# A hybrid attention encoder: half of the third branch's attention weights are transposed by VectorE and a DRAM round trip, the other half where they lie

## The chip, the cores and the metric

The kernel runs on one core of a Trainium2 chip. The metric is the device time of one launch in microseconds (us), the median of three runs. A core has five engines with an instruction queue each: TensorE (PE), VectorE (DVE), ScalarE (ACT), GpSimd (POOL) and SyncE (SP). SP does nothing here but issue DMAs. Engines meet only at semaphores, and each runs its own instructions strictly in order.

## The reference

Two layers over a sequence of 512 tokens with 1024 channels. Each layer normalizes x, projects it, runs three token mixers side by side, gates and merges them, and adds the result to x. The second and the third mixer turn attention weights:

```python
# B: differential attention, 4 heads of two maps each
s = einsum('bhtqd,bhtkd->bhtqk', qblk, k) * scale
p = softmax(s, axis=-1)
w = p[:, :, 0] - lam * p[:, :, 1]
o = einsum('bhqk,bhke->bhqe', w, v)
# C: dilated windows, 8 heads; three patterns (window, dilation),
# each a masked softmax, merged by a softmax over the three log-sums
s = where(valid, s, -1e30)
lse = logsumexp(s, axis=-1); p = exp(s - lse[..., None])
wts = softmax(stack(lses), axis=0)
o_c = einsum('gbhs,gbhsd->bhsd', wts, stack(outs))
```

The merge of C equals one softmax over all 512 keys whose scores carry the logarithm of how many patterns see the key; the kernel computes it so, with a mask of logarithms (`lmask`).

## The kernel before

Each layer has three stages: the norm of x, four *groups* of heads, then the branch and output projections. A group i holds one GLA head, one B head and two C heads, and 18 tiles of the input projection: four of values (`v0` to `v3`), `a`, `bq` to `ck`, the gates `ag`, `bg`, `cg` and the merge gates `m0` to `m5`. The first group of a layer is written out and the other three run in a loop, so a layer's groups hold the same work. A product in full precision is three matmuls of rounded parts (high times high, high times low, low times high), so a tile of 128 x 512 is 8 steps of 3 matmuls.

PE's order is written out by hand. Behind `bg`, the seven tiles `cg` to `m5` are cut into 56 *filler steps* (`fill(n)` issues n of them), and they stand between the pieces of attention so that PE has work while other engines go through the softmax. The attention of a group is 16 score blocks j of 128 queries x 512 keys: j = 0 to 7 are B's (two maps for each of four query blocks), j = 8 to 15 are C's (two heads for each of four blocks). `scores(p)` makes j = 2p and 2p+1 in the banks `score0` and `score1`. DVE takes the row maximum (`row_max`; for C it also adds `lmask` and leaves the negated scores in `sneg`, two buffers), ACT the exponential with its row sum into `probs` (`exp`, four buffers inside the tile `six`), DVE divides by the sum (`weights`). The result is one of 12 *weight units* u of 128 queries x 512 keys: u = 0 to 3 for B, 4 to 11 for C, two buffers in `w`. Queries lie on the partitions and the product with the values needs keys there, so PE turns each unit (`turn_weights`: four transposes of 128 x 128 into a PSUM bank) and ACT copies it out (`turned`) into `wt`, for C's second head into `wt1`. These two are halves of `big`. `values` then makes the heads' outputs at the end of the group: 4 x 2 matmuls of 64 output rows into `mbank`. Where the program counts unit u, block j is u + 4 for C.

ACT also evaluates the gates (`merge_gate(m)` reads the finished tile, frees its PSUM bank for the tile after next, and stores it to DRAM), and the two norms' inverse roots: Ln, then Exp, each behind a table load (`rr`, signalled by `r_done`). DVE multiplies both outputs by them (L1020, L1021). At the end of a layer DVE makes the low parts `yl` of all 12 outputs (L1033), which the branch projection needs.

SP streams the weight tiles into three slots. Each load waits until POOL has split the tile that used the slot (L417 and L426), and POOL waits until PE has finished the tile that used the split slot.

## Time and profile before

| what | value |
|---|---|
| median of 3 runs | 1241.05 us (1240.67 to 1241.31) |
| the profiled execution | 1237.68 us |
| its span | 1235.9 us |
| granted PE clock, mean | 0.996 |
| a group in the loop, on PE | 120.6 us |
| DMA | 148.62 MB, 120 GB/s |

The profile is of one execution, 3.4 us faster than the median. The period of a group is the distance between equal instructions of two groups in the chain of waits (the last products of two groups start at 261.00 and 381.62 us). The eight groups take some 965 of the 1236 us. A matmul's shown duration is longer than the distance to the next, since they are pipelined: distances between starts say what one costs.

### The profile page before, as it was taken

The numbers are of one execution on the slowest core, as the hardware profiler recorded it, in microseconds if no ns is written. First come the engines' busy times: TensorE is split into PE (matmuls) and PEld (weight loads), VectorE is DVE, ScalarE is ACT, GpSimd is POOL, SyncE is SP. The second block draws the span as 40 slices with busy tenths as digits, with TensorE's granted clock in tenths as the row PEclk, the third lists the DMA queues.
The fourth block names the chain that finished last, engine by engine and source line by source line (L and its number), as shares of the span: only waits on it lengthen the run. The fifth ranks groups of instructions, "written<-read, shape, count | busy, mean of one in ns | idle before, by whom it ended". The sixth has DMA issues, their size and how long they took to land.

```text
span 1235.9 us, 17632 instructions
## 1 busy us (share of the span) xinstructions
PE 1210.9 (98%) x5840; PEld 984.2 (80%) x5840; DVE 695.7 (56%) x1037; ACT 441.9 (36%) x799; POOL 832.1 (67%) x595
## 2 busy tenths in 40 slices
PE   7999999999999999999999999999999999999995
PEld 5877888788878887787888778887887798777884
DVE  6686327532753385677658841583247335648842
ACT  6425523542454235100253453145324532450012
POOL 5787377638762976677749753885488548757881
PEclk9999999999999999999999999999999999999998
DMA  6333233323332333374244222523252314336611
GB/s 241 103 119 113 94 103 109 106 94 113 100 104 93 119 102 129 125 256 154 90 155 145 86 105 77 170 79 107 73 153 90 116 56 148 102 107 232 204 69 68
DMA packets 52079, 148.62 MB, mean 120 GB/s; under 512 B 6848, under 2 KB 8384, under 8 KB 51648
## 3 DMA queue, kind: packets, MB, share of 16 engines
q1 hardware_dynamic: 29088, 103.04, 24.0%
q10 hardware_dynamic: 22944, 44.98, 12.0%
q8 instruction: 25, 0.41, 0.1%
q14 instruction: 22, 0.18, 0.0%
HBM read 114.45 MB, written 16.78 MB: 106 GB/s over the span
## 4 chain that ended last, share of the span: by engine, by line
PE 93%; DVE 3%; DMA 1%; ACT 1%; ACTq 1%; issue 1%; POOLq 0%; POOL 0%; DVEq 0%
PE proj L1098 53%; PE proj L1202 10%; PE turn L1337 4%; PE turn L1263 3%; PE score L1337 3%; PE score L1255 3%; PE score L1256 2%; PE mbank L1271 2%; PE obank L1271 2%; PE mbank L1337 2%; PE obank L1337 2%; PE proj L1116 1%; PE obank L1290 1%; DMA big<-big 1%; DVE yl L1033 1%; PE mbank L1090 1%
## 5 line engine op out<-in xcount | busy, mean ns | idle before, releaser
L426 POOL TENSOR_TENSOR wl<-raw_w,wh 128x512 fp32r<-128x512 f32 x352 | 503.9, 1452 | 31.7 <-POOL wh L417 31.7
L417 POOL TENSOR_SCALAR wh<-raw_w 128x1024 fp32r<-128x1024 f32 x176 | 215.4, 1224 | 284.6 <-issue 101.9
L1098 PE MATMUL proj<-hh,wh 128*128 128x512 f32 x1024 | 405.6, 396 | 0.5 <-DVE big L1060 0.5
L1098 PE MATMUL proj<-hh,wl 128*128 128x512 f32 x1024 | 400.5, 391 | 0.0
L1098 PE MATMUL proj<-hl,wh 128*128 128x512 f32 x1024 | 399.5, 390 | 0.0
L1098 PEld LDWEIGHTS proj<-hh,wl 128*128 128x128 f32 x1024 | 192.2, 188 | 41.8
L1098 PEld LDWEIGHTS proj<-hh,wh 128*128 128x128 f32 x1024 | 192.4, 188 | 41.0 <-issue 1.3
L1098 PEld LDWEIGHTS proj<-hl,wh 128*128 128x128 f32 x1024 | 192.5, 188 | 39.2
L536 ACT ACTIVATE six<-big 128x512 f32<-128x512 f32 x24 | 15.0, 626 | 202.9 <-DVE big L1060 202.9
L949 DVE CUSTOM_DVE_ANT_0 six<-score,lmask 128x512 f32<-128x512 f32 x64 | 43.2, 684 | 66.3 <-PE score L1256 66.3
L907 DVE TENSOR_TENSOR group<-big,group 128x512 f32<-128x512 f32 x24 | 37.5, 1613 | 71.7 <-ACT big L633 71.4
L721 ACT ACTIVATE big<-turn 128x512 f32<-128x512 f32 x96 | 56.1, 593 | 59.8 <-PE turn L1263 59.0
L713 ACT ACTIVATE six<-score,negmax 128x512 f32<-128x512 f32 x64 | 43.5, 685 | 81.5 <-DVE negmax L943 81.5
L1202 PE MATMUL proj<-wh,hh 128*128 128x384 f32 x192 | 64.8, 337 | 0.0
L1202 PE MATMUL proj<-wh,hl 128*128 128x384 f32 x192 | 64.2, 334 | 0.0
L1202 PE MATMUL proj<-wl,hh 128*128 128x384 f32 x192 | 64.1, 334 | 0.0
L1255 PE MATMUL score<-yh 128*128 128x512 f32 x128 | 56.5, 442 | 3.5 <-DVE group L938 3.5
L351 POOL TENSOR_TENSOR yh<-big,yh 64x1024 fp32r<-64x1024 f32 x16 | 38.3, 2396 | 31.7 <-ACT yh L656 30.3
L713 ACT ACTIVATE six<-six,negmax 128x512 f32<-128x512 f32 x64 | 46.0, 718 | 31.3 <-DVE negmax L949 31.3
L1263 PE MATMUL turn<-ident,w 128*128 128x128 f32 x384 | 56.3, 272 | 0.0
L1263 PEld LDWEIGHTS turn<-ident,w 128*128 128x128 f32 x384 | 46.5, 139 | 10.5
L616 ACT ACTIVATE big<-proj 128x512 f32<-128x512 f32 x32 | 19.2, 599 | 95.4 <-PE proj L1098 95.2
(205 smaller groups left out, 1886.8 us busy)
## 6 DMA issues: line engine op xcount, KB each, us to landing
raw_w<-weights SPq DMA_DIRECT2D x175, 512.0 KB, 3.3
gate_scratch<-gstage ACTq DMA_DIRECT2D x48, 256.0 KB, 2.0
six<-gate_scratch ACTq DMA_DIRECT2D x16, 768.0 KB, 5.4
big<-big ACTq DMA_DIRECT2D x64, 128.0 KB, 4.2
yh<-yh ACTq DMA_DIRECT2D x64, 128.0 KB, 2.4
big<-x_t SPq DMA_DIRECT2D x4, 512.0 KB, 6.6
big<-x_t SPq DMA_DIRECT2D x1, 2048.0 KB, 8.9
x_scratch<-big SPq DMA_DIRECT2D x1, 2048.0 KB, 7.3
```

Of the source, the lines that this page charges most:

```text
L351: return eng.tensor_tensor(yh[other, q_of(n, head):low_of(n, head) + 1:4, :], t[own, 0:2, :], yh[own, q_of(n, head):high_of(n, head) + 1:2 ...
L417: pool.tensor_scalar(wh[:, slot, :, :], src, 1.0, 1.0, ALU.mult, ALU.mult).then_inc(pool_high.sem, 1)
L426: ins = pool.tensor_tensor(wl[:, slot, half, :], src[:, half, :], wh[:, slot, half, :].bitcast(F32), ALU.subtract)
L713: act.activation(probs[:, j % 4, :], src, ACT.Exp, bias=negmax[:, j:j + 1], scale=k, accum_out=sums[:, j:j + 1]).then_inc(exp_done.sem, 1)
L721: act.activation((wt if u < 4 or u % 2 == 0 else wt1)[:, :, q:q + P], turn[u % 2][:, :].rearrange("p (k q) -> p k q", k=QB), ACT.Copy).the ...
L949: dve.tensor_tensor_reduce(sneg[:, j % 2, :], score[j % 2][:, :], lmask[:, S - P - P * b:2 * S - P - P * b], -1.0, 3.0e38, ALU.add, ALU.mi ...
L1098: last = pe.matmul(dst, a[:, slot, k, :], b[:, k, :], start=(k == 0 and a is wh and b is hh), stop=(k == KT - 1 and a is wl))
L1202: last = pe.matmul(proj[b % 2][:, 0:3 * P], a(k)[:, P * b:P * b + P], c[:, 0:3, k, :], start=(k == 0 and n == 0), stop=(k == KT - 1 and n ...
L1255: pe.matmul(score[head][:, :], yh[:, q_of(n, head), q], yh[:, high_of(n, head), :], start=True, stop=False)
L1263: last = pe.transpose(turn[u % 2][:, P * k:P * k + P], w[:, u % 2, P * k:P * k + P], ident[:, :])
L1271: last = pe.matmul(dst, v[:, k, cols], weights[:, k, :], start=(k == 0), stop=(k == QB - 1))
L1337: last = pe.matmul(zbanks[zt % 6][:, :], a[:, SLOT[c % BRANCH_SLOTS], n, :], (yl if is_low else yh)[:, b, :], start=(k == 0 and a is wh an ...
```

## The change

C's blocks are reordered: j = 8 to 11 are now the first head's four query blocks, j = 12 to 15 the second head's.

The first head's units (`VIA` = 4 to 7) leave PE. DVE makes only the reciprocal of the sum (`inverse`), ACT scales the exponentials in place (`scale`), DVE transposes within blocks of 32 x 32 into `w` (`turn_32`), and SP sends each pair of units to a scratch tensor in DRAM (`send`: four DMAs, each of 32 partitions, 512 runs of 64 elements) and brings it back with the blocks in their places in `wt1` (`bring`: four DMAs with runs of 256 elements). `turn_32(6)` writes the buffer that the first `send` reads, and waits for it (`w_free`). The tokens come back in an order in which pairs of query blocks are interleaved in pieces of 32, so the last product on DVE is cut into four pieces of 64 x 128 and one of 64 x 512.

The second head's units (8 to 11) are scaled in place and turned by PE out of `probs`, without `w`. They go to `wt`.

ACT, DVE and PE have a new order in the second half of a group, and the filler steps are dealt out anew; their number is the same.

```diff
+VIA = list(range(4,8))
+BY_PE = [u for u in range(12) if u not in VIA]
...
+        def by_quarter(t, n):
+
+            return t.rearrange("p n s -> p (n s)").rearrange("p (c k n j) -> p k c n j", c=4, k=QB, n=2)[:, :, :, n, :]
+
...
+        def weights_used(G, u):
+
+            return turned_32.at(G, VIA.index(u) + 1) if u in VIA else w_ready.at(G, BY_PE.index(u) + 1)
+
+        def w_free(G, u):
+
+            if u in VIA:
+                m = VIA.index(u) // 2
+                return sent.at(G, 64 * m) if m else turn_done.at(G, len([n for n in BY_PE if n < u]))
+            return turn_done.at(G, BY_PE.index(u - 2) + 1)
+
...
+            def send(G, m):
+
+                sp.wait_ge(*turned_32.at(G, 2 * m + 2))
+                for a in range(4):
+                    sp.dma_start(turned_d[m, :, :, a, :], w[32 * a:32 * a + 32, :, :].rearrange("i n s -> i (n s)").rearrange(
+                        "i (x j) -> i x j", j=64)).then_inc(sent.sem, 16)
+
+            def bring(G, m):
+
+                u = VIA[2 * m]
+                if u == 4:
+                    sp.wait_ge(*c_parts.at(G, 1))
+                    apart(sp)
+                sp.wait_ge(*sent.at(G, 64 * (m + 1)))
+                k, q = (0 if u >= 4 else QB), 2 * P * (u % 4 // 2)
+                for c in range(4):
+                    sp.dma_start(big[32 * c:32 * c + 32, k:k + QB, q:q + 2 * P], turned_d[m, :, QB * c:QB * c + QB, :, :].rearrange(
+                        "i x a j -> i x (a j)")).then_inc(back.sem, 16)
...
+                        if j == 15:
+                            send(L * NG + i, 0)
+                    bring(L * NG + i, 0)
+                    send(L * NG + i, 1)
+                    bring(L * NG + i, 1)
...
+                    def scale(u):
+
+                        j = 2 * u if u < 4 else u + 4
+                        act.wait_ge(*rs_ready.at(G, VIA.index(u) + 1))
+                        act.activation(probs[:, j % 4, :], probs[:, j % 4, :], ACT.Copy, scale=rs[:, j:j + 1]).then_inc(scaled.sem, 1)
...
-                    for u in range(4, 10):
-                        exp(u + 6)
-                        turned(u)
-                        if u == 5:
-                            merge_gate(2)
-
-                            act.wait_ge(*out_done.at(G, 2))
-                            grp.did(act.activation(rr[:, 0, :], mbank[:, :], ACT.Ln, bias=cst[:, 0:1]))
-                            act.wait_ge(*out_done.at(G, 4))
-                            grp.did(act.activation(rr[:, 1, :], obank[:, :], ACT.Ln, bias=cst[:, 0:1]))
-                            grp.last()
-                            act.activation(rr[:, :, :], rr[:, :, :], ACT.Exp, scale=-0.5).then_inc(r_done.sem, 1)
-                        if u == 7:
-                            merge_gate(3)
-                        if u == 9:
-                            merge_gate(4)
+                    scale(4)
+                    exp(10)
+                    scale(5)
+                    exp(11)
+                    merge_gate(2)
+                    scale(6)
+                    exp(12)
+                    scale(7)
+                    exp(13)
+                    act.wait_ge(*out_done.at(G, 2))
+                    grp.did(act.activation(rr[:, 0, :], mbank[:, :], ACT.Ln, bias=cst[:, 0:1]))
+                    act.wait_ge(*out_done.at(G, 4))
+                    grp.did(act.activation(rr[:, 1, :], obank[:, :], ACT.Ln, bias=cst[:, 0:1]))
+                    grp.last()
+                    act.activation(rr[:, :, :], rr[:, :, :], ACT.Exp, scale=-0.5).then_inc(r_done.sem, 1)
+                    turned(8)
+                    turned(9)
+                    merge_gate(3)
+                    exp(14)
+                    exp(15)
                     turned(10)
+                    merge_gate(4)
                     turned(11)
...
+                    def inverse(u):
+                        if u < 4:
+                            a, c = 2 * u, 2 * u + 1
+                            dve.wait_ge(*exp_done.at(G, c + 1))
+                            grp.did(dve.reciprocal(rs[:, a:a + 2], sums[:, a:a + 2]))
+                            grp.last()
+                            dve.tensor_scalar(rs[:, c:c + 1], rs[:, c:c + 1], sc[:, 2:3], None, ALU.mult).then_inc(rs_ready.sem, 1)
+                        else:
+                            j = u + 4
+                            dve.wait_ge(*exp_done.at(G, j + 1))
+                            dve.reciprocal(rs[:, j:j + 1], sums[:, j:j + 1]).then_inc(rs_ready.sem, 1)
+
+                    def turn_32(u):
+                        j = 2 * u if u < 4 else u + 4
+                        dve.wait_ge(*scaled.at(G, VIA.index(u) + 1))
+                        if u < 4:
+                            dve.wait_ge(*rs_ready.at(G, VIA.index(u) + 1))
+                            grp.did(dve.scalar_tensor_tensor(probs[:, j % 4, :], probs[:, (j + 1) % 4, :], rs[:, j + 1:j + 2], probs[:, j % 4, :],
+                                                             ALU.mult, ALU.add))
+                            grp.last()
+                        if u >= 2:
+                            dve.wait_ge(*w_free(G, u))
+                        dve.transpose(by_quarter(w[:, :, :], u % 2), probs[:, j % 4, :].rearrange("p (k c j) -> p k c j", k=QB, c=4)).then_inc(turned_32.sem, 1)
...
-                    weights(4)
+                    inverse(4)
                     row_max(10)
+                    turn_32(4)
                     dve.wait_ge(*sq_done.at(G, 2))
                     dve.wait_ge(*sq_high_done.at(G, 2))
                     dve.tensor_tensor(sq_low, sqb[:, :], sq_high.bitcast(F32), ALU.subtract).then_inc(sq_low_done.sem, 1)
                     dve.scalar_tensor_tensor(y[:, NG + i, :], obank[:, :], sc[:, 4:5], sg[:, 1, :], ALU.mult, ALU.mult).then_inc(y_read.sem, 1)
-                    for u in range(5, 12):
-                        weights(u)
-                        if u < 10:
-                            row_max(u + 6)
-                        if u == 8:
-                            dve.wait_ge(*r_done.at(G, 1))
-                            dve.wait_ge(*y_read.at(G, 2))
-                            grp.did(dve.tensor_tensor(y[:, i, :], y[:, i, :], rr[:, 0, :], ALU.mult))
-                            dve.tensor_tensor(y[:, NG + i, :], y[:, NG + i, :], rr[:, 1, :], ALU.mult).then_inc(ab_normed.sem, 1)
+                    inverse(5)
+                    row_max(11)
+                    turn_32(5)
+                    inverse(6)
+                    row_max(12)
+                    row_max(13)
+                    turn_32(6)
+                    inverse(7)
+                    turn_32(7)
+                    weights(8)
+                    row_max(14)
+                    weights(9)
+                    row_max(15)
+                    dve.wait_ge(*r_done.at(G, 1))
+                    dve.wait_ge(*y_read.at(G, 2))
+                    grp.did(dve.tensor_tensor(y[:, i, :], y[:, i, :], rr[:, 0, :], ALU.mult))
+                    dve.tensor_tensor(y[:, NG + i, :], y[:, NG + i, :], rr[:, 1, :], ALU.mult).then_inc(ab_normed.sem, 1)
+                    weights(10)
+                    weights(11)
                     dve.wait_ge(*out_done.at(G, 5))
-                    dve.scalar_tensor_tensor(y[:, 2 * NG + i, :], mbank[:, :], 0.5, sg[:, 2, :], ALU.mult, ALU.mult).then_inc(y_read.sem, 1)
+                    h0, h1 = rows_of(0), rows_of(1)
+                    for b in range(QB):
+                        dve.scalar_tensor_tensor(tokens(y[h0, 2 * NG + i, :], b), by_token(mbank[h0, :], b), 0.5, tokens(sg[h0, 2, :], b), ALU.mult, ALU.mult)
+                    dve.scalar_tensor_tensor(y[h1, 2 * NG + i, :], mbank[h1, :], 0.5, sg[h1, 2, :], ALU.mult, ALU.mult).then_inc(y_read.sem, 1)
...
-                        n, b = p // 4, p % 4
-                        q = slice(P * b, P * b + P)
-
-
-                        for head in range(2):
-                            pe.matmul(score[head][:, :], yh[:, q_of(n, head), q], yh[:, high_of(n, head), :], start=True, stop=False)
-                            pe.matmul(score[head][:, :], yh[:, q_of(n, head), q], yh[:, low_of(n, head), :], start=False, stop=True).then_inc(score_done.sem, 1)
+                        n = p // 4
+                        for half in range(2):
+
+                            head, b = (half, p) if n == 0 else ((p - 4) // 2, 2 * (p % 2) + half)
+                            q = slice(P * b, P * b + P)
+                            pe.matmul(score[half][:, :], yh[:, q_of(n, head), q], yh[:, high_of(n, head), :], start=True, stop=False)
+                            pe.matmul(score[half][:, :], yh[:, q_of(n, head), q], yh[:, low_of(n, head), :], start=False, stop=True).then_inc(score_done.sem, 1)
 
                     def turn_weights(u):
-                        pe.wait_ge(*w_ready.at(G, u + 1))
-                        if u >= 2:
-                            pe.wait_ge(*wt_ready.at(G, u - 1))
+                        turned = BY_PE.index(u)
+                        pe.wait_ge(*w_ready.at(G, turned + 1))
+                        if turned >= 2:
+                            pe.wait_ge(*wt_ready.at(G, turned - 1))
                         for k in range(QB):
-                            last = pe.transpose(turn[u % 2][:, P * k:P * k + P], w[:, u % 2, P * k:P * k + P], ident[:, :])
+                            part = w[:, u % 2, P * k:P * k + P] if u < 4 else probs[:, u % 4, P * k:P * k + P]
+                            last = pe.transpose(turn[u % 2][:, P * k:P * k + P], part, ident[:, :])
...
-                    values(4, out_done, (obank[:, :], slice(P, 2 * P), wt))
-                    for u in range(4, 10):
-                        if u % 2 == 0:
-                            scores(u // 2 + 3)
-                        fill(3 if u in (5, 7) else 4)
-                        turn_weights(u)
-                        if u == 5:
-                            pe.wait_ge(*y_read.at(G, 2))
-                            mean_of(obank, 2)
+                    pe.wait_ge(*wt_ready.at(G, 4))
+                    values(out_done, (obank[:, :], slice(P, 2 * P), wt))
+                    scores(5)
+                    fill(6)
+                    pe.wait_ge(*y_read.at(G, 2))
+                    mean_of(obank, 2)
+                    scores(6)
                     fill(4)
+                    scores(7)
+                    fill(3)
+                    turn_weights(8)
+                    fill(2)
+                    turn_weights(9)
+                    fill(8)
                     turn_weights(10)
+                    fill(2)
                     turn_weights(11)
-                    fill(3)
+                    fill(4)
                     assert filled == KT * len(FILLERS)
                     pe.wait_ge(*r_done.at(G, 1))
-                    values(12, out_done, (mbank[0:HD, :], slice(2 * P, 2 * P + HD), wt),
-                           (mbank[HD:P, :], slice(2 * P + HD, 3 * P), wt1))
+                    pe.wait_ge(*back.at(G, PAIRS * 64))
+                    pe.wait_ge(*wt_ready.at(G, len(BY_PE)))
+                    values(out_done, (mbank[0:HD, :], slice(2 * P, 2 * P + HD), wt1),
+                           (mbank[HD:P, :], slice(2 * P + HD, 3 * P), wt))
```

On DVE, in the first group of a layer, from the maximum of block 10 on. Before (L988 is the reciprocal, L990 the scaling, L949 the maximum with its read-out, L1011 and L1012 the squares' low part and the product for B):

```order
L949 ISA six,negmax<-score,lmask 128x512
L949 ISA negmax 128x1
L1011 TENSOR_TENSOR yl<-group,yl 128x512
L1012 SCALAR_TENSOR_TENSOR y<-obank,sc,group 128x512
L988 RECIPROCAL rs<-sums 128x1
L990 TENSOR_SCALAR w<-six,rs 128x512
L949 ISA six,negmax<-score,lmask 128x512
L949 ISA negmax 128x1
L988 RECIPROCAL rs<-sums 128x1
L990 TENSOR_SCALAR w<-six,rs 128x512
L949 ISA six,negmax<-score,lmask 128x512
L949 ISA negmax 128x1
```

After (L1074 and L1060 are the reciprocals, L1021 the maximum, L1086 the transpose in blocks of 32, L1062 the scaling in place):

```order
L1086 STREAM_TRANSPOSE w<-six 128x4x4x32
L1074 RECIPROCAL rs<-sums 128x1
L1021 ISA six,negmax<-score,lmask 128x512
L1021 ISA negmax 128x1
L1021 ISA six,negmax<-score,lmask 128x512
L1021 ISA negmax 128x1
L1086 STREAM_TRANSPOSE w<-six 128x4x4x32
L1074 RECIPROCAL rs<-sums 128x1
L1086 STREAM_TRANSPOSE w<-six 128x4x4x32
L1060 RECIPROCAL rs<-sums 128x1
L1062 TENSOR_SCALAR six<-six,rs 128x512
```

Two maxima stand together ahead of the third transpose, and both of the last transposes stand ahead of the first scaling that PE waits for.

On ACT, the same stretch. Before (L713 is the exponential, L721 the copy of a turned unit, L704 and L706 a merge gate and its store, L755 to L759 the roots):

```order
L713 ACTIVATE six,sums<-six,negmax 128x512
L721 ACTIVATE big<-turn 128x4x128
L704 ACTIVATE gstage<-proj 128x512
L706 DMA gate_scratch<-gstage 128x512
L755 ACT_TABLE_LOAD
L755 ACTIVATE group<-mbank,cst 128x512
L757 ACTIVATE group<-obank,cst 128x512
L759 ACT_TABLE_LOAD
L759 ACTIVATE group<-group 128x1024
L713 ACTIVATE six,sums<-six,negmax 128x512
L721 ACTIVATE big<-turn 128x4x128
```

After (L789 is the new scaling, L774 the exponential, L825 to L829 the roots, L782 the copy of a turned unit, L765 a merge gate):

```order
L789 ACTIVATE six<-six,rs 128x512
L774 ACTIVATE six,sums<-six,negmax 128x512
L825 ACT_TABLE_LOAD
L825 ACTIVATE group<-mbank,cst 128x512
L827 ACTIVATE group<-obank,cst 128x512
L829 ACT_TABLE_LOAD
L829 ACTIVATE group<-group 128x1024
L782 ACTIVATE big<-turn 128x4x128 x2
L765 ACTIVATE gstage<-proj 128x512
L767 DMA gate_scratch<-gstage 128x512
L774 ACTIVATE six,sums<-six,negmax 128x512 x2
```

The roots stand behind block 13's exponential now, and the first two copies of turned units and a merge gate behind them; the exponentials of blocks 14 and 15 come last.

On SP, at the end of a group's loads, after (L403 is a weight load, L410 a send, L422 a bring; before, the two weight loads stood next to each other and the group ended with them):

```order
L403 DMA raw_w<-weights 128x1024
L408 ISA
L410 DMA turn_scratch<-w 512x1x64 x4
L444 REGISTER_ALU
L403 ISA
L403 DMA raw_w<-weights 128x1024
L419 ISA
L422 DMA big<-turn_scratch 32x4x256 x4
L408 REGISTER_ALU
L410 DMA turn_scratch<-w 512x1x64 x4
L419 REGISTER_ALU
L422 DMA big<-turn_scratch 32x4x256 x4
```

The last weight load of a group and everything that the next group loads stand behind waits for DVE.

## Rows read from the trace of the kernel before

**Rows 1.** The page's part 1: busy us (share of the span) xinstructions.

```profile
PE 1210.9 (98%) x5840; PEld 984.2 (80%) x5840; DVE 695.7 (56%) x1037; ACT 441.9 (36%) x799; POOL 832.1 (67%) x595
```

**Rows 2.** Waits of PE: engine line <- releaser: us in total, times, longest.

```profile
PE mbank L1090 <- ACT six L536: 7.6, 1, 7.6
PE score L1255 <- DVE group L938: 3.5, 2, 2.0
```

**Rows 3.** The page's part 5 (line, engine, out<-in, count | busy us, mean ns).

```profile
L1263 PE MATMUL turn<-ident,w 128*128 128x128 f32 x384 | 56.3, 272 | 0.0
```

**Rows 4.** Timeline of PE, the fourth group: start us, us, instruction, count.

```profile
474.88 0.79 PE L1255 MATMUL score<-yh 128*128 128x512 f32 x1
...
492.72 0.60 PE L1263 MATMUL turn<-ident,w 128*128 128x128 f32 x4
493.08 0.48 PE L1098 MATMUL proj<-hh,wh 128*128 128x512 f32 x1
...
495.94 0.60 PE L1263 MATMUL turn<-ident,w 128*128 128x128 f32 x4
...
502.18 3.65 PE L1271 MATMUL mbank<-big,group 128*64 128x512 f32 x16
```

**Rows 5.** Timeline of ACT and its DMA issues (ACTq), the same group.

```profile
433.82 2.91 ACTq L680 DMA_DIRECT2D big<-big  x4
...
475.98 0.59 ACT L747 ACTIVATE yl<-obank 128x512 fp32r<-128x512 f32 x1
...
483.76 1.28 ACT L755 ACT_TABLE_LOAD   x1 [0.54 <-ACT gstage L704]
...
488.60 0.71 ACT L713 ACTIVATE six<-six,negmax 128x512 f32<-128x512 f32 x1
...
491.72 0.34 ACTq L706 DMA_DIRECT2D gate_scratch<-gstage  x1
```

**Rows 6.** Timeline of DVE, the same group.

```profile
476.13 0.69 DVE L949 CUSTOM_DVE_ANT_0 six<-score,lmask 128x512 f32<-128x512 f32 x1 [6.08 <-PE score L1256]
...
477.86 0.74 DVE L1012 SCALAR_TENSOR_TENSOR y<-obank,sc,group 128x512 f32 x1
...
479.91 0.49 DVE L990 TENSOR_SCALAR w<-six,rs 128x512 f32<-128x512 f32 x1
...
489.69 1.35 DVE L990 TENSOR_SCALAR w<-six,rs 128x512 f32<-128x512 f32 x1
...
506.01 0.69 DVE L1023 SCALAR_TENSOR_TENSOR y<-mbank,group 128x512 f32 x1 [8.76 <-PE mbank L1271]
```

**Rows 7.** Timeline of POOL, the same group.

```profile
488.25 1.04 POOL L417 TENSOR_SCALAR wh<-raw_w 128x1024 fp32r<-128x1024 f32 x1 [4.00 <-issue]
489.48 2.74 POOL L426 TENSOR_TENSOR wl<-raw_w,wh 128x512 fp32r<-128x512 f32 x2 [0.18 <-POOL wh L417]
```

**Rows 8.** The page's part 6: DMAs, count, KB each, us from issue to landing.

```profile
raw_w<-weights SPq DMA_DIRECT2D x175, 512.0 KB, 3.3
gate_scratch<-gstage ACTq DMA_DIRECT2D x48, 256.0 KB, 2.0
...
big<-big ACTq DMA_DIRECT2D x64, 128.0 KB, 4.2
```

**Rows 9.** The page's part 3: queue, packets, MB, share of 16 engines.

```profile
q1 hardware_dynamic: 29088, 103.04, 24.0%
q10 hardware_dynamic: 22944, 44.98, 12.0%
```

**Rows 10.** Windows (us; PEclk, DMA share, GB/s come last).

```profile
960.90:961.15 0.25, 0.25 (x3) 0.21 (x2) 0.21 (x3) 0.00 (x0) 0.00 (x0) 1.00 1.53 279
466.50:467.00 0.50, 0.50 (x4) 0.41 (x3) 0.50 (x1) 0.00 (x0) 0.50 (x1) 1.00 1.00 385
```

**Rows 11.** Chain of waits: start us, us, what.

```profile
506.91 3.87 DVE yl L1033 x7
...
1188.56 32.94 PE proj L1098 x144
```

More of the change, by code:

```diff
@@ L137, in low_of, with steps_of_weights, build @@
     return 6 * n + 4 + head
+def steps_of_weights():
+    return sum(2 if u in VIA else 3 for u in range(4)) + sum(1 for u in range(4, 12) if u not in VIA)
 def unit_of(j):
     return j // 2 if j < 8 else j - 4
-def build(nc, x_d, w_d, par_d, up_d, gain_d, cos_d, sin_d, lmask_d, cmask_d, gmask_d, ident_d, out_d, gate_d, xkeep_d):
+def build(nc, x_d, w_d, par_d, up_d, gain_d, cos_d, sin_d, lmask_d, cmask_d, gmask_d, ident_d, out_d, gate_d, xkeep_d, turned_d):
     with ExitStack() as ctx:
@@ L243, in build @@
         score_done = sig("score_done", 16)
-        turn_done = sig("turn_done", 12)
+        turn_done = sig("turn_done", len(BY_PE))
         out_done = sig("out_done", 5)
@@ L264, in build @@
         exp_done = sig("exp_done", 16)
-        wt_ready = sig("wt_ready", 12, 1)
+        wt_ready = sig("wt_ready", len(BY_PE), 1)
+        scaled = sig("scaled", len(VIA))
         sq_done = sig("sq_done", 2)
@@ L289, in build @@
         max_ready = sig("max_ready", 16)
-        w_ready = sig("w_ready", 12)
+        w_ready = sig("w_ready", len(BY_PE))
+        rs_ready = sig("rs_ready", len(VIA))
+        turned_32 = sig("turned_32", len(VIA))
         y_read = sig("y_read", 3, 1)
@@ L293, in build @@
         s_mean = sig("s_mean", 0)
-        dve_grp = sig("dve_grp", 35)
+        dve_grp = sig("dve_grp", 15 + steps_of_weights())
         ab_normed = sig("ab_normed", 1)
@@ L309, in build @@
         pool_high = sig("pool_high", ROWS_LAYER)
+        sent = sig("sent", PAIRS * 64)
+        back = sig("back", PAIRS * 64)
         swapped = sig("swapped", 2 * 64)
@@ L352, in low_parts, with by_token, tokens @@
                                      yh[own, q_of(n, head):high_of(n, head) + 1:2, :].bitcast(F32), ALU.subtract)
+        def by_quarter(t, n):
+            return t.rearrange("p n s -> p (n s)").rearrange("p (c k n j) -> p k c n j", c=4, k=QB, n=2)[:, :, :, n, :]
+        def by_token(t, b):
+            pair = t[:, 2 * P * (b // 2):2 * P * (b // 2) + 2 * P]
+            return pair.rearrange("p (a n j) -> p a n j", a=4, n=2)[:, :, b % 2, :]
+        def tokens(t, b):
+            return t[:, P * b:P * b + P].rearrange("p (a j) -> p a j", a=4)
+        def weights_used(G, u):
[5 more added lines that the diff above has]
+            return turn_done.at(G, BY_PE.index(u - 2) + 1)
         def apart(eng):
@@ L944, in row_max @@
                         else:
-                            b = (j - 8) // 2
+                            b = j % 4
                             if j >= 10:
@@ L1470 @@
     x_scratch = nc.dram_tensor("x_scratch", (P, KT, S), F32, kind="Internal").ap()
-    build(nc, *args, out, gate_scratch, x_scratch)
+    turn_scratch = nc.dram_tensor("turn_scratch", (PAIRS, 32, 16, 4, 64), F32, kind="Internal").ap()
+    build(nc, *args, out, gate_scratch, x_scratch, turn_scratch)
     r = run(nc, [arrays], core_ids=[0])
```

20 lines of the change are left out of this document (10 added, 10 removed).

## The prediction

> **What bounds the kernel.** I read the busy shares first, then PE's waits, then one group on the timelines of PE, ACT and DVE, and last the DMA rows. PE is busy 98% of the span; VectorE and ScalarE stand at 56% and 36% [rows 1]. PE's waits for other engines come to some 12 us, all at the start of the launch and in the first group of a layer [rows 2]. Inside a group PE never waits: a filler step of three matmuls costs 3 x 32.94 / 144 = 0.686 us [rows 11], which is the distance of matmuls fed without a gap. So work taken from PE is time won at full price, and every new wait of PE is time lost at full price. The eight groups are alike, so everything below is worked out for one group, on the clock of the fourth group, and taken eight times.
>
> **What PE loses.** The turns of units 4 to 7: 4 x 4 of the 48 transposes of a group. Their price is not the mean of 272 ns, and not quite the 56.3 us over 384 of the busy column (147 ns) either [rows 3]. From one turn's start to the next, 492.72 to 495.94, lie the turn and four filler steps: 3.22 - 4 x 0.686 = 0.48 us for a unit, which takes in that the first matmul behind a turn is longer [rows 4]. The same from 495.94 to 502.18 with three turns and seven steps: 6.24 - 4.80 = 1.44, again 0.48. The gain is 4 x 0.48 = 1.92 us a group, **15.4 us** in all. Scores, steps, products with the values and the eight other turns stay.
>
> **What the other engines get, and when.** ScalarE swaps four copies out of PSUM (0.6 us) for four scalings in place, which the trace doesn't show; I take 0.65, between that copy and the exponential of 0.71 [rows 5]. VectorE gives up four scalings of 0.49 and gets four transposes, also not shown; the nearest rows are one-pass operations on 128 x 512 at 0.69 to 0.74 [rows 6]. I take 0.7, with 0.5 and 1.35 (the same scaling when it meets POOL's split) as ends. Then the walk, all from starts that the change leaves alone:
>
> - scores(5) starts at 474.88 as before. Four matmuls at 0.23, the first 0.4 longer, end the piece at 476.2 [rows 4]. Six steps give 480.3, the two matmuls of the mean 480.8, scores(6) 481.7, four steps 484.5, scores(7) 485.4, three steps **487.4**: here PE wants unit 8.
> - ScalarE finishes the squares at 476.57 [rows 5] and scale(4) at 477.2. VectorE: maximum 10 to 476.8, turn_32(4) to 477.9, the low part and the product for B (0.7 each) to 479.2, the reciprocal and maximum 11 to 480.0 [rows 6]. That lets scores(6) go at 480.8 with 0.8 us to spare, and the mean at 480.3 with 1.1. scale(5) is done at 480.0, turn_32(5) at **480.75**.
> - SP has long issued the load ahead of it and sends pair 0. Call X the time from 480.75 until all four DMAs have landed. Maxima 12 and 13 are taken meanwhile (to 483.0), so scores(7) isn't held up. But turn_32(6) writes the buffer that is being sent, and VectorE stands there until 480.75 + X. Behind it in the queue: the fourth reciprocal 0.15, scale(7) on ScalarE 0.65, turn_32(7) 0.7, and reciprocal and scaling of unit 8, 0.7, with turn_32(6) itself 0.7 and the hand-overs 0.05. Sum **2.95 us**. PE waits for all of it.
> - PE's wait at unit 8 is therefore X + 2.95 - 6.65 = X - 3.7. Next, ScalarE's roots: from the table load at 483.76 to the next instruction at 488.60 it takes 4.84 us [rows 5]; with the copies, gate and exponentials in order, unit 10 is ready 10.85 us after the landing, while PE, if it waited at unit 8, comes to it 2.95 + 3 x 0.48 - 0.48 + 10 x 0.686 = 10.77 after. That is 0.1 more. For a scaling that meets POOL's split, which starts around 488.25 [rows 7] and made one scaling 1.35 instead of 0.49 [rows 6], I add 0.2. The new wait is **X - 3.4**, not below nothing.
>
> **X, the unknown.** No row has 256-byte runs. Below: a store of 256 KB to DRAM lands 2.0 us after its issue [rows 8] and issues cost 0.34 each [rows 5], so 3 x 0.34 + 2.0 = 3.0. Above: over 16 engines and 1235.9 us, q10's 12.0% for 22,944 packets is 0.103 us for one of 1.96 KB, q1's 24.0% for 29,088 is 0.163 us for one of 3.54 KB [rows 9]; the line through both is 0.029 + 0.038 for each KB, so 0.039 for 256 bytes. A send is 2048 packets, 128 an engine: 5.0 us. With one issue, and the 2.0 - 8 x 0.103 = 1.2 us of a store that isn't packet time, 6.5. But packets of an engine overlap: a window shows a DMA share of 1.53 [rows 10], and then 5.0 becomes 3.3 and X 4.8. I take the middle of 3.0 and 4.8, **3.9**: the store is the nearest row (same direction, same queue kind), and its 2.0 us hardly varies. A quarter of the exchange `big<-big` has the same 32 partitions and 128 KB; it lands in 4.2 with issues of 0.73 [rows 5, 8], up to 6.4 for four, yet those go into SBUF beside weight loads.
>
> The wait is then 0.5 us a group, **4 us** in all.
>
> The Trainium skill speaks against this change here. "DMA: Bandwidth & Descriptors", Specifications, says that line rate needs at least 512 bytes and that below it the DMA does a read-modify-write. No run here shows that yet. If each run cost as a packet of 512 bytes with its share of fixed time, some 0.048 us, X would be 7.6 instead of 3.9 and the sum below would turn to +20.
>
> **What is hidden.** The return: pair 1 is turned 2.3 us behind the landing, sent in X and brought in 4 to 5, so it is back at about 487 + 2X = 495; PE wants it at 487.4 + 0.5 + 4 x 0.48 + 16 x 0.686 = 500.8. Loads behind SP's waits: the group's last weight load goes at 482 and is split when m4 is done, near 495; the next group's first loads wait for pair 1's bring at about 480.75 + 2X + 4 = 493 and its tiles come after 28 us of value tiles. A load takes 3.3 us [rows 8]. The 16.8 MB of added traffic is 11% on top. POOL's work is the same.
>
> **What isn't hidden.** The last product on DVE was one of 0.69 us [rows 6]; four pieces of 64 x 128 and one of 64 x 512 should take 1.6 to 1.7. In a group nobody waits for it. At a layer's end seven low parts stand in the chain right behind it [rows 11], so both layers pay 0.9: **1.8 us**.
>
> **Sum.** -15.4 + 4.0 + 1.8 = -9.6 us: the profiled execution's 1237.68 becomes 1228.1, the median 1241.05, 3.4 above it, **1231.5**. With X = 3.0: -13.6, and -15.4 if the tail costs nothing: 1226. What this measurement can tell from no change is about 0.2%, 2.5 us.
>
> **Rivals.**
>
> 1. *The send is slow, slower than before.* Its place is turn_32(6), in front of everything VectorE does for PE. At X = 6.5 the wait is 3.1 us a group, 24.8 in all: -15.4 + 24.8 + 1.8 = +11.2, **1252**. It decides from X = 5.1 on, where the wait of 1.7 eats 15.4 - 1.8. For it: 2048 small packets, and the exchange's 4.2 to 6.4. Against: the store's steady 2.0 and overlapping packets.
> 2. *The gain goes almost all into the wait.* X = 4.4 to 5.5: -5.6 to +3.2, about **1240**. Every tenth of a microsecond of VectorE's transposes above 0.7 counts about four times before PE's unit 8, so transposes at 1.0 us with X = 3.9 come to the same place.
> 3. *The return is late or the next group starves.* PE stops before the last product. It needs X above 8, or a bring that waits behind gate stores; +1 us a group on the forecast gives **1239.5**.
> 4. *The change doesn't free what the turns seem to cost*, because the shown distance was weight loading that the scores and steps next to them now carry. With 147 ns a transpose instead of 120 it would even be more; with half of 0.48, 7.7 less: **1239**.
>
> **Chances.** Forecast 0.50 (X 3.0 to 4.4); rival 1 0.24; rival 2 0.16; rival 3 0.05; rival 4 0.05. Faster by over 0.2%: the forecast, half of rival 2 and part of 3 and 4, 0.60. Within 0.2%: 0.09. Slower: rival 1 and the upper end of rival 2, 0.31. The range goes from 1226 to 1251: it leaves out the slow half of rival 1. The forecast's own range is 1226 to 1236.
>
> **What would show it.** PE's waits should have a new row, turn <- DVE's scaling of unit 8 (L1062), eight times some 0.3 us, and one of about 0.1 to 0.2 at unit 10. Sends land 2.9 us behind their issue; DVE's transpose is 0.7 us; the idle time ahead of it at turn_32(6), from 483.0 on, is 1.7 us. A group's period goes from 120.6 to 119.2. If instead that idle time is over 3 us, rival 1 has it; if PE waits for a DMA into `big`, rival 3. The forecast is wrong if the period is 120 or more.

## The result and the profile after

The changed kernel takes **1252.2 us** (median of 4, 1250.0 to 1253.9) against 1241.2 (median of 4): a ratio of 1.0092, 95% interval 1.0079 to 1.0106, so 11 us slower. The forecast was 1231.5, with a range from 1226 to 1251. 1252 is the figure of rival 1.

The busy shares have hardly moved. The sixteen transposes of a group are gone from PE (5840 to 5712 matmuls), and its busy time fell by 2 us only [rows 1, 3]:

```profile
PE 1208.7 (97%) x5712; PEld 977.1 (78%) x5712; DVE 697.6 (56%) x1069; ACT 444.3 (36%) x799; POOL 833.4 (67%) x595
```

PE's waits have a new first row, for VectorE's scaling in place (L1062), of 16.8 us in 11 pieces; the long ones at the start are the old ones [rows 2]:

```profile
PE turn L1375 <- DVE six L1062: 16.8, 11, 3.0
PE mbank L1200 <- ACT six L597: 7.6, 1, 7.6
PE score L1365 <- DVE group L1010: 1.8, 1, 1.8
```

The same stretch of PE's timeline as [rows 4], in the fourth group, which is 4 us later on the clock. The columns are start, duration, instruction and, in brackets, the idle time before it and what ended it:

```profile
493.28 0.66 PE L1375 MATMUL turn<-ident,six 128*128 128x128 f32 x4 [1.90 <-DVE six L1062]
...
501.46 0.66 PE L1375 MATMUL turn<-ident,six 128*128 128x128 f32 x4 [0.21 <-DVE six L1062]
...
506.64 2.79 PE L1382 MATMUL mbank<-big,group 128*64 128x512 f32 x12
```

Unit 8's turn waits 1.90 us, unit 10's 0.21. The time from the start of B's product (`obank`) to the start of the last product (`mbank`) will serve as the measure of a group's second half. The chain of waits shows it (start, duration, what) for this group and for the third, which is slower for a reason that comes below:

```profile
475.78 3.45 PE obank L1382 x8
...
506.71 3.61 PE mbank L1382 x16
```

```profile
353.30 3.45 PE obank L1382 x8
...
385.37 3.58 PE mbank L1382 x16
```

That is 30.93 and 32.07 us. The period of a group is 121.3 to 122.5 us, where it was 120.6 and should have become 119.2.

VectorE in this stretch, to be set beside [rows 6]. The rows are the second, third and fourth transpose in blocks of 32, unit 8's scaling and, at the layer's end, the last product in pieces:

```profile
483.87 0.71 DVE L1086 STREAM_TRANSPOSE w<-six 128x512 f32<-128x512 f32 x1 [0.19 <-ACT six L789]
...
490.40 0.71 DVE L1086 STREAM_TRANSPOSE w<-six 128x512 f32<-128x512 f32 x1 [3.67 <-DMA turn_scratch<-w]
...
491.95 0.71 DVE L1086 STREAM_TRANSPOSE w<-six 128x512 f32<-128x512 f32 x1 [0.79 <-ACT six L789]
...
492.74 0.49 DVE L1062 TENSOR_SCALAR six<-six,rs 128x512 f32<-128x512 f32 x1
...
510.48 0.87 DVE L1132 SCALAR_TENSOR_TENSOR y<-mbank,group 64x128 f32 x4 [7.61 <-PE mbank L1382]
511.37 0.69 DVE L1133 SCALAR_TENSOR_TENSOR y<-mbank,group 64x512 f32 x1
```

X, the time from the end of the second transpose (484.58) to the landing that releases the third (490.40), is 5.8 us, and the third transpose waited 3.67 us for the send; over 3 us was the prediction's sign for rival 1. From the start of the third transpose to unit 8's turn on PE it is 490.40 to 493.28, 2.88 us. SP beside it (queue, DMA, count; the duration is that of all issues together):

```profile
484.61 3.36 SPq L410 DMA_DIRECT2D turn_scratch<-w  x4
...
490.32 1.76 SPq L422 DMA_DIRECT2D big<-turn_scratch  x4
```

The DMA rows, to be set beside [rows 8]:

```profile
gate_scratch<-gstage ACTq DMA_DIRECT2D x48, 256.0 KB, 2.8
...
turn_scratch<-w SPq DMA_DIRECT2D x64, 128.0 KB, 3.2
big<-turn_scratch SPq DMA_DIRECT2D x64, 128.0 KB, 2.9
```

A DMA of a send lands 3.2 us after its issue (median), where I had 2.0 from the gate's store, which itself takes 2.8 now. And the four of the first send take 3.36 us to issue, 0.84 each, where I had 0.34. The chain of waits has the last of the four from its issue to its landing:

```profile
487.02 3.28 DMA turn_scratch<-w
```

So X is 2.4 us of issues ahead of the last one, 3.3 us for the last, and 0.1 of hand-overs.

The clock is the second part of the result. Windows of 1 us in the third group. Behind the stretch stand its length and the busy shares of PE, its weight loads, VectorE, ScalarE and POOL; the last three columns are the granted clock, the DMA share and GB/s:

```profile
370.00:371.00 1.00, 0.22 (x2) 0.22 (x3) 0.96 (x4) 0.98 (x3) 0.82 (x2) 1.00 0.93 245
371.00:372.00 1.00, 1.00 (x8) 0.86 (x7) 0.96 (x4) 0.99 (x2) 1.00 (x2) 0.99 0.59 145
372.00:373.00 1.00, 1.00 (x4) 0.81 (x3) 0.76 (x3) 0.98 (x3) 1.00 (x1) 0.50 0.70 159
373.00:374.00 1.00, 1.00 (x7) 0.80 (x5) 0.00 (x0) 1.00 (x1) 0.28 (x1) 0.50 0.94 204
```

PE stood for 1.87 us up to 370.78, and from 371.97 on the granted clock is 0.50 of full speed, the 1.2 GHz level of the two (1.2 and 2.4), for 3.4 us. Two matmuls are 0.43 us apart there instead of 0.23. This happened in five of the eight groups of the profiled execution, behind waits of 1.85 to 1.90 us in four and of 3.03 us in one. The other three (the first, second and fourth) stayed at 1.00 behind waits of 1.76 to 1.91 us. Before, no group had it.

### The profile page after: what moved, and what is told of

It is laid out like the page before. It is cut to its first block, busy times and chain, and to the rows that moved or that the text cites. A ratio compares the mean times of both kernels' runs of the same rounds, so it can differ in the third digit from the quotient of the medians.

```text
span 1249.8 us, 17434 instructions
## 1 busy us (share of the span) xinstructions
PE 1208.7 (97%) x5712; PEld 977.1 (78%) x5712; DVE 697.6 (56%) x1069; ACT 444.3 (36%) x799; POOL 833.4 (67%) x595
## 4 chain that ended last, share of the span: by engine, by line
PE 82%; DVE 5%; ACT 4%; issue 3%; DMA 3%; SPq 1%; ACTq 1%; POOLq 0%; POOL 0%; DVEq 0%
PE proj L1208 47%; PE proj L1312 9%; PE turn L1455 4%; PE score L1455 3%; PE mbank L1382 2%; PE turn L1375 2%; PE obank L1382 2%; DMA turn_scratch<-w 2%; PE mbank L1455 2%; PE obank L1455 2%; PE score L1365 2%; SPq L410 1%; PE score L1366 1%; PE proj L1226 1%; ACT six L789 1%
## 5 line engine op out<-in xcount | busy, mean ns | idle before, releaser
L487 POOL TENSOR_TENSOR wl<-raw_w,wh 128x512 fp32r<-128x512 f32 x352 | 505.1, 1455 | 31.7 <-POOL wh L478 31.7
L1021 DVE CUSTOM_DVE_ANT_0 six<-score,lmask 128x512 f32<-128x512 f32 x64 | 42.6, 683 | 58.7 <-PE score L1366 58.7
L774 ACT ACTIVATE six<-score,negmax 128x512 f32<-128x512 f32 x64 | 43.5, 685 | 81.6 <-DVE negmax L1015 81.6
L1365 PE MATMUL score<-yh 128*128 128x512 f32 x128 | 55.9, 437 | 2.8 <-DVE group L1010 1.8
L774 ACT ACTIVATE six<-six,negmax 128x512 f32<-128x512 f32 x64 | 45.7, 714 | 23.9 <-DVE negmax L1021 18.7
L984 DVE TENSOR_TENSOR big<-big,cos 128x1024 f32<-128x1024 f32 x8 | 13.5, 1684 | 66.8 <-DMA big<-big 66.8
L1366 PE MATMUL score<-yh 128*128 128x512 f32 x128 | 50.5, 394 | 0.0
L1015 DVE TENSOR_REDUCE negmax<-score 128x1 f32<-128x512 f32 x64 | 41.0, 682 | 12.1 <-PE score L1366 11.8
```

Of the source, the lines that this page charges most:

```text
L487: ins = pool.tensor_tensor(wl[:, slot, half, :], src[:, half, :], wh[:, slot, half, :].bitcast(F32), ALU.subtract)
L774: act.activation(probs[:, j % 4, :], src, ACT.Exp, bias=negmax[:, j:j + 1], scale=k, accum_out=sums[:, j:j + 1]).then_inc(exp_done.sem, 1)
L1015: dve.tensor_reduce(negmax[:, j:j + 1], score[j % 2][:, :], AX_X, ALU.max, negate=True).then_inc(max_ready.sem, 1)
L1021: dve.tensor_tensor_reduce(sneg[:, j % 2, :], score[j % 2][:, :], lmask[:, S - P - P * b:2 * S - P - P * b], -1.0, 3.0e38, ALU.add, ALU.mi ...
L1365: pe.matmul(score[half][:, :], yh[:, q_of(n, head), q], yh[:, high_of(n, head), :], start=True, stop=False)
L1366: pe.matmul(score[half][:, :], yh[:, q_of(n, head), q], yh[:, low_of(n, head), :], start=False, stop=True).then_inc(score_done.sem, 1)
```

## The experiments

Each ratio is against the kernel before, taken beside the run: 1240.4 us for the first four experiments, 1239.2 for the last four, and 1241.2 for the changed kernel. So a difference between an experiment and the changed kernel's 1252.2 has up to 2 us in it that may be the chip's. The first four are one family: what is it that makes PE wait?

**The second head first.** VectorE's order alone:

```diff
                     row_max(13)
-                    turn_32(6)
                     inverse(7)
+                    weights(8)
+                    weights(9)
+                    turn_32(6)
                     turn_32(7)
-                    weights(8)
                     row_max(14)
-                    weights(9)
                     row_max(15)
```

> VectorE's order is changed alone: the fourth reciprocal and the scalings of units 8 and 9 (the head that PE turns) stand ahead of the third and fourth transposes, which wait for the send. Theory A (PE stood at unit 8 because VectorE stood behind the send's buffer, and PE's clock fell behind that idle time in five of eight groups): PE's 1.9 us ahead of unit 8 and the 0.2 ahead of unit 10 go, the granted clock stays at 1.00 in every group, a group takes 120.6 - 1.9 = 118.7 us, and the median falls from 1252.2 to 1227 to 1229. Rival B (the added DMA traffic or the longer queues slow the kernel by themselves): PE still waits or its work is slower, above 1240. Rival C (the four turns never cost 0.48 us each): no waits, yet 1231 to 1236.

**1225.6 us** (1224.9 to 1226.0), ratio 0.9884 (0.9867 to 0.9900): faster than both kernels, and 1.4 us below the range of theory A. PE has no wait for a turn of the second head, and the clock stays at 1.00 in the groups. VectorE's rows, the fourth group again:

```profile
478.82 0.53 DVE L1062 TENSOR_SCALAR six<-six,rs 128x512 f32<-128x512 f32 x1
...
480.14 0.49 DVE L1062 TENSOR_SCALAR six<-six,rs 128x512 f32<-128x512 f32 x1
481.93 1.30 DVE L1086 STREAM_TRANSPOSE w<-six 128x512 f32<-128x512 f32 x2 [1.29 <-DMA turn_scratch<-w]
```

The scalings of units 8 and 9 are done at 479.35 and 480.63, and only then does VectorE stand for the send (1.29 us). PE's time from the start of B's product to the start of the last product, here and in the kernel before:

```profile
467.29 3.43 PE obank L1382 x8
...
495.67 3.61 PE mbank L1382 x16
```

```profile
472.01 3.43 PE obank L1271 x8
...
502.25 3.61 PE mbank L1271 x16
```

It is 28.38 against 30.24 us: four turns are worth 1.86 us, 0.465 each. Rivals B and C fall.

**Two buffers.** The same goal by another way, with the changed kernel's orders:

```diff
+        w_second = group[:, 6:8, :]
...
-                return sent.at(G, 64 * m) if m else turn_done...
+                return back.at(G, 0) if m else turn_done...
...
-                        dve.transpose(by_quarter(w[:, :, :], u % 2), ...
+                        dve.transpose(by_quarter((w_second if u >= 6 else w)[:, :, :], u % 2), ...
```

> The second pair is transposed into a part of the tile group that is free by then (the slots cum and rest) instead of w, so the third transpose no longer waits for the send; the order of every engine is the changed kernel's. Theory A: VectorE's 3.7 us of idle time ahead of the third transpose go, unit 8 is ready at least 1 us before PE wants it, the median is 1227 to 1229, the same as with the other order. Rival B: above 1240. If only a part of the wait goes, because block 14 or the roots are then late, some 0.5 to 1 us a group stay: 1231 to 1237.

1225.6 us (1224.9 to 1226.2). The third transpose writes `group`, and starts the moment the maximum ahead of it ends; unit 8 is scaled at 480.85:

```profile
478.03 0.71 DVE L1087 STREAM_TRANSPOSE group<-six 128x512 f32<-128x512 f32 x1
...
479.57 0.71 DVE L1087 STREAM_TRANSPOSE group<-six 128x512 f32<-128x512 f32 x1 [0.79 <-ACT six L790]
...
480.36 0.49 DVE L1063 TENSOR_SCALAR six<-six,rs 128x512 f32<-128x512 f32 x1
```

Both ways land within 0.1 us of each other. What cost the time was that VectorE stood behind the buffer, with PE's unit 8 behind that in its queue. The traffic and the transposes are all still there.

**Long runs.** The same bytes from the same partitions, in runs of 4 KB:

```diff
-                    sp.dma_start(turned_d[m, :, :, a, :], w[32 * a:32 * a + 32, :, :]... "i (x j) -> i x j", j=64)
+                    sp.dma_start(turned_d[m, 8 * a:8 * a + 8, ...].rearrange("(i e) -> i e", i=32),
+                                 w[32 * a:32 * a + 32, :, :].rearrange("i n s -> i (n s)"))
```

> Each of the four DMAs of a send writes 32 runs of 4 KB instead of 512 runs of 256 bytes (the blocks then don't come back in their places, so the output isn't the reference's; bytes, partitions, waits and the bring are the same). Theory A1 (the small runs make the send slow): its issue falls from 0.64 to 0.35 us and its landing from 3.2 to 2.2, so that X, the time from the second transpose to the last landing, falls from 5.8 to 3.4 us, PE's wait at unit 8 goes: 1227 to 1231. Rival A2 (a DMA from 32 partitions is slow to issue and land whatever its runs, as the exchange in big with 0.6 to 0.7 and 3.7 to 4.2 us): X stays at 5 to 5.8 and the median at 1245 to 1252.

1242.5 us (1240.3 to 1243.6), between the two theories. Four issues take 2.34 us instead of 3.36, while the last DMA of the send takes as long as before (3.45 us against 3.28):

```profile
483.50 2.34 SPq L410 DMA_DIRECT2D turn_scratch<-w  x4
```

From the end of the second transpose (483.46) to the third (488.36) it is now 4.9 us, 0.9 less:

```profile
482.75 0.71 DVE L1086 STREAM_TRANSPOSE w<-six 128x512 f32<-128x512 f32 x1 [0.20 <-ACT six L789]
...
488.36 0.71 DVE L1086 STREAM_TRANSPOSE w<-six 128x512 f32<-128x512 f32 x1 [2.75 <-DMA turn_scratch<-w]
...
490.69 1.08 DVE L1062 TENSOR_SCALAR six<-six,rs 128x512 f32<-128x512 f32 x1
```

So the runs of 256 bytes are 0.9 us of the 5.8, and A1 fails for the rest. PE's wait for L1062 falls from 16.8 to 12.4 us, and behind none of these waits, of up to 1.58 us, does the clock fall. (It does once elsewhere, at the first group's first scores, behind a wait of 1.85 us.) Unit 8's scaling took 1.08 us in this group, which gives back part.

**Steps moved.** PE's order alone:

```diff
-                    fill(3)
+                    fill(5)
                     turn_weights(8)
                     fill(2)
                     turn_weights(9)
-                    fill(8)
+                    fill(6)
```

> Two of the eight filler steps between units 9 and 10 stand ahead of unit 8 (5, 2, 6 instead of 3, 2, 8). Units 8 and 10 are ready at the same times as before the edit, so the idle time of PE is the same 2.1 to 2.4 us a group in sum, but split: some 0.5 at unit 8 and 1.6 at unit 10. Theory A alone (idle time is what costs): 1252 stays, within 1.5. With the clock as a part of its own (idle time of 1.9 us in one piece is what it falls behind): fewer of the eight groups show a granted clock of 0.50, and the median falls by up to 5.6 us, to 1246.5.

1246.7 us (1245.7 to 1246.8): 5.6 less than the changed kernel, or 4.8 if each is set against its own kernel before (+6.3 and +11.0). The waits are nearly as long in sum, but in three pieces a group. The third, which I had not foreseen, is for the PSUM bank that a merge gate frees (L765):

```profile
PE turn L1375 <- DVE six L1062: 11.0, 16, 0.9
...
PE proj L1208 <- ACT gstage L765: 4.7, 8, 0.6
```

11.0 + 4.7 is 15.7 against 16.8 us. From B's product to the last a group takes 30.9 to 31.1 us, against 30.8 to 31.0 in the changed kernel's groups at full clock, 32.1 in four of those where it fell, and 33.2 in the fifth. The clock is at 1.00 in all eight groups, here in the third behind unit 8's turn:

```profile
371.00:372.00 1.00, 0.46 (x4) 0.28 (x4) 0.96 (x4) 0.98 (x2) 0.82 (x2) 1.00 0.82 241
372.00:373.00 1.00, 1.00 (x8) 0.87 (x7) 0.96 (x4) 0.99 (x3) 1.00 (x2) 1.00 0.58 146
```

With this the clock's share is shown: about 5 to 6 us. It is not measured quite alone: the fifth group lost its extra 1.1 us of waiting as well, while the groups took 0.1 to 0.3 us more than those at full clock had.

The next three test what X consists of, and how it reaches PE. For them X is again the time from the end of the second transpose to the landing.

**One DMA.**

```diff
-                for a in range(4):
-                    sp.dma_start(turned_d[m, :, :, a, :], w[32 * a:32 * a + 32, :, :]...)
+                sp.dma_start(turned_d[m, ...].rearrange("i x a j -> a i x j"), w[:, :, :]... "p (x j) -> p x j", j=64)
```

> A send is one DMA from all 128 partitions with the same 2048 runs of 256 bytes, instead of four of 32 partitions; waits and orders as in the changed kernel. With long runs X (from the end of the second transpose to the last landing) had fallen only from 5.8 to 4.9 us, so most of it must be elsewhere. Theory I (four issues of 0.64 us one behind the other, plus one landing): X falls to about 4.0, PE's wait at unit 8 to 0.1 to 0.5 us, no group has a granted clock of 0.50, median 1233 to 1239. Rival J (an issue takes as long as it has runs to describe): one issue takes 2 to 2.6 us, X stays at 5 to 5.8, 1244 to 1252.

1316.2 us (1312.4 to 1319.3), outside of both. The issue is short, 0.57 us, which refutes J; but X is 11.0 us, so theory I's figure fails too, and PE waits over 7 us in each group:

```profile
507.19 0.57 SPq L409 DMA_DIRECT2D turn_scratch<-w  x1
...
518.19 1.76 SPq L421 DMA_DIRECT2D big<-turn_scratch  x4
```

While it runs, the DMA engines are busy for 0.31 and move 71 GB/s:

```profile
513.00:514.00 1.00, 0.96 (x5) 0.46 (x3) 0.00 (x0) 0.00 (x0) 0.00 (x0) 1.00 0.31 71
```

That is the busy time of 5 of 16 engines. This one DMA doesn't keep them all busy. Its outer count in DRAM is 4; that this decides was not tried by itself. The rate is useful all the same: 71 GB/s in 256-byte pieces over 0.31 x 16 = 5 engines is 18 ns for a packet, where I had drawn a line to 39. So 128 packets an engine are 2.3 us, not 5.0.

**Sent twice.**

```diff
-                for a in range(4):
-                    sp.dma_start(turned_d[m, :, :, a, :], ...
+                for copy, a in [(c, a) for c in (1, 0) for a in range(4)]:
+                    sp.dma_start(turned_d[m + PAIRS * copy, :, :, a, :], ...
```

> The suspected cost doubled: each send stores its pair twice, into two places, eight DMAs instead of four. Theory A: what makes X longer makes PE's wait longer by as much. If the issues set X, four more of 0.64 to 0.84 us add 2.6 to 3.4 us to X and to PE's wait at unit 8 in each group; the pair's return is then up to 6 us later as well, which comes on top at the last product if it is late there; with the clock at 0.50 in all groups: 1276 to 1300. Rival B (PE's wait has another cause than the send): 1252 to 1257.

1283.4 us (1281.7 to 1284.0), as theory A has it, and the clock falls in all eight groups. The eight issues take 6.33 us, and X is 498.20 to 506.74, 8.5 us, 2.7 more than with four:

```profile
498.23 6.33 SPq L410 DMA_DIRECT2D turn_scratch<-w  x8
```

```profile
497.49 0.71 DVE L1086 STREAM_TRANSPOSE w<-six 128x512 f32<-128x512 f32 x1 [0.20 <-ACT six L789]
...
506.74 0.71 DVE L1086 STREAM_TRANSPOSE w<-six 128x512 f32<-128x512 f32 x1 [6.40 <-DMA turn_scratch<-w]
```

PE's wait grew from 1.90 to 4.62 us, by the same 2.7. So X is issues, here about 0.7 us for each one added, and one landing behind the last: 2.4 + 3.3 us in the changed kernel, 1.3 + 3.5 with long runs, 5.7 + 2.8 here (issues ahead of the last DMA, and that DMA from issue to landing).

**The maximum behind.** One part of the change undone:

```diff
                     row_max(12)
-                    row_max(13)
                     turn_32(6)
+                    row_max(13)
```

> One part of the change undone: the maximum of block 13 stands behind the third transpose, which waits for the send, and not ahead of it. The fourth pair of score products of the second half (blocks 14 and 15) needs this maximum. Theory A: PE waits at these products until the send has landed, plus transpose and maximum, some 3.5 us, and then nowhere else: 1.2 us a group more than the 2.1 of now, and the clock at 0.50 in all eight groups: 1262 to 1267. Rival (VectorE's order around the maxima doesn't matter, as its share of busy time is 56%): 1252, within 2.

1268.6 us (1268.1 to 1269.7), 1.6 above the range of theory A. PE waits at the scores now, 8 times, 3.1 to 3.4 us, and the clock falls to 0.50 behind seven of them; unit 8's turn waits for nothing:

```profile
499.19 0.79 PE L1365 MATMUL score<-yh 128*128 128x512 f32 x1 [3.38 <-DVE negmax L1021]
...
504.90 0.60 PE L1375 MATMUL turn<-ident,six 128*128 128x128 f32 x4
```

The position of that maximum ahead of the third transpose is worth 16 us (18 against each one's own kernel before); VectorE's 56% of busy time says nothing on it.

**The product whole.** On the order with the second head first:

```diff
-                    for b in range(QB):
-                        dve.scalar_tensor_tensor(tokens(y[h0, ...], b), by_token(mbank[h0, :], b), 0.5, ...)
-                    dve.scalar_tensor_tensor(y[h1, ...], mbank[h1, :], 0.5, ...)
+                    dve.scalar_tensor_tensor(y[:, 2 * NG + i, :], mbank[:, :], 0.5, sg[:, 2, :], ...)
```

> On the order with the second head first (1225.6 us): the last product of a group is one instruction of 128 x 512 again instead of four of 64 x 128 and one of 64 x 512 (the tokens of one head are then not put back in order, so the output isn't the reference's). The prediction priced the pieces at 0.9 us for each of the two layer ends, 1.8 in all. By that term: 1223.8. If the tail is shorter, since PE has work of its own there: 1224.5 to 1225.5. In the inner groups nothing changes.

1224.4 us (1223.6 to 1225.9) against 1225.6. The medians show nothing: each is 14.8 to 14.9 us below its own kernel before. The chains of waits do. From the start of the last product of a layer to PE's work on the branch products behind it, with the pieces and with the product whole:

```profile
495.67 3.61 PE mbank L1382 x16
...
506.68 5.65 PE turn L1455 x24
```

```profile
495.88 3.61 PE mbank L1379 x16
...
506.00 5.65 PE turn L1452 x24
```

That is 11.01 against 10.12 us, and at the second layer's end 11.02 against 10.12: the pieces cost 0.9 at each, as the prediction had it.

## Why the prediction was wrong

The mechanism was rival 1's. That its number, 1252, was met as well is luck: it had X at 6.5 and 24.8 us of waits and knew of no clock; X was 5.8 and the waits cost some 20 us, and the clock made up the rest. The forecast took the wrong size for one term and had no term for another.

- *PE is the bound, and every wait counts in full.* Right. PE's wait and X moved together (1.90 and 5.8, 4.62 and 8.5), and there was none in the two kernels where PE's units didn't stand behind the send.
- *The turns are worth 15.4 us.* Right: 8 x 1.86 = 14.9 us.
- *The walk to 480.75 and the chain of 2.95 us behind the send.* Right: the second transpose ends at 484.58, which is 480.81 on the clock of before, and the chain is 2.88. The transpose is 0.71 (I had 0.7), the scaling on ScalarE 0.72 (0.65).
- ***X = 3.9 us* is the step that failed.** It was 5.8. My lower bound was 1.0 us of issues and 2.0 for a landing, both from the gate's store; the runs showed 2.4 and 3.3, with an issue at 0.84 on average and at 0.7 for each of four more. Of my two bounds I took the middle. The exchange `big<-big`, 0.73 an issue and 4.2 to land [rows 5, 8], has the same partitions and bytes, and it gives 6.4 for four. It was the nearest row, and I set it aside for its direction. With long runs X was still 4.9. In the other direction I had the packets' own time too long (39 against 18 ns). The Trainium skill's 512-byte rule ("DMA: Bandwidth & Descriptors", Specifications) was worth at most the 0.9 us that longer runs saved, not 3.7. With X = 5.8 my formula gives a cost of 2.4 us a group. In the three groups at full clock I find 30.90 on average, less 28.38: 2.5. Over eight groups that is 20.2 us instead of 4.
- *A scaling that meets POOL's split, 0.2.* About right as a mean: one group of eight showed it. In the fifth the scaling took 1.43 us instead of 0.49, and PE waited 3.03. POOL's split (L487) had started 0.11 us ahead of it:

```profile
735.56 1.43 DVE L1062 TENSOR_SCALAR six<-six,rs 128x512 f32<-128x512 f32 x1
```

```profile
735.45 2.67 POOL L487 TENSOR_TENSOR wl<-raw_w,wh 128x512 fp32r<-128x512 f32 x2 [0.18 <-POOL wh L478]
```

- *The clock.* The sum had no term for it. Where PE stood some 1.9 us and more in one piece, the clock mostly fell to 0.50 for 3.4 us. Four of these five groups took 32.1 us where those at full clock took 30.9, so it costs 1.16 us a time and 5.8 in all. (The loss of half of 3.4 us would be 1.7; a part comes back, since unit 10 then no longer makes PE wait.)
- *The tail, 1.8.* Right: from the start of the last product to the branch products it is 10.13 us before and 11.02 after, at both layer ends.
- *What is hidden* stayed hidden: PE never waited for a return or for weights.

Sum with the measured sizes: -14.9 + 20.2 + 1.1 (the fifth group) + 5.8 + 1.8 = 14.0 us, against 13.9 between the two spans. Two small differences that nearly cancel aren't explained: the first group's attention was 0.6 us later, and the stretches behind the layer ends were 0.3 and 0.5 us shorter. The profiled execution before was a fast one, so the medians are only 11 us apart.

## What to carry to other kernels

When work goes from the engine that bounds to a chain through DRAM, ask first who stands behind the wait for the transfer's source buffer, and put what the bounding engine needs ahead of it: the same instructions in that order gained 15 us where they had lost 11. Price a transfer that is cut into several DMAs by its issues, taken from a row with the same partitions, plus one landing. And if PE must wait, deal out its work so that it waits in short pieces: here three pieces of 0.5 to 0.9 us a group cost little beyond themselves, while behind one of 1.9 us the clock mostly fell, for another 1.2 us.

## What the runs showed of the hardware

- A DMA out of 32 partitions cost its queue 0.64 us (median; 0.84 on average in a group's first send) to issue in runs of 256 bytes and 0.42 (median; 0.59 on average in the first send) in runs of 4 KB; the returns, runs of 1 KB, 0.43.
- One DMA with 2048 runs of 256 bytes and an outer count of 4 moved 71 GB/s with the busy time of about 5 of 16 engines, and landed after 11 us; the same bytes in four DMAs had landed after 5.8.
- VectorE's transpose of 128 x 512 float32 in blocks of 32 x 32 takes 0.71 us, 32 times within 0.004; the scaling of the same size, 0.49 in most places, took 1.43 where POOL's split had started just ahead of it.
- In the changed kernel the lower clock followed PE's waits at unit 8 in five of eight groups (1.85 to 1.90 us, and one of 3.03), but not waits of 1.76, 1.90 and 1.91 us. With the maximum behind, it followed seven of eight waits of 3.1 to 3.4 us. In the groups of no run here did it follow a wait of up to 1.6 us.
